# Differential attention in 512-column projections, with two-group turning and six weight low parts on GpSimd

## The chip, the cores and the metric

One core of one Trainium2 chip runs the whole program. The metric is the device time of one execution in microseconds (us). The engines are TensorE (PE; its weight loads are shown apart as PEld), VectorE (DVE), ScalarE (ACT), GpSimd (POOL) and SyncE (SP), which issues the weight transfers.

## What is computed

The program computes one 256-token sequence of width 1024 through three layers: a hybrid layer, then a layer with gated linear attention, then one with differential attention; each of the last two has a gated feed-forward block and a gated embedding step behind it. Only the mixer of the third layer is changed. Cut to that:

```
q, k, v = split(h @ w_in)                      # w_in 1024 x 3072: 1024 columns each
q = rope(rms_norm(q per 64 columns, g_q))      # 8 heads x 2 maps x 64 columns
k = rope(rms_norm(k per 64 columns, g_k))
lam = exp(sum(lam_q1*lam_k1)) - exp(sum(lam_q2*lam_k2)) + lambda_init
pr = softmax(q k^T / 8)                        # two maps for each head
a = pr[0] - lam * pr[1]
o = rms_norm(a @ v per head, g_sub) * (1 - lambda_init)
return o @ w_out                               # w_out 1024 x 1024
```

## The kernel before

All matrix products run at f32 accuracy as three fp32r products. A weight chunk of 1 MB (128 partitions x 2048 values) lands in a slot of RAW. ACT rounds it into WH, the high part (`hi`, line 1129), then DVE subtracts it from RAW into WL, the low part (`lo`, line 1730, two inputs from SBUF). PE then adds high by high, high by low and low by high (`mm3`; line 375 is the matmul of all of them, line 383 the transpose). RAW, WH and WL have three slots each. Chunk c is fetched when both parts of c-3 are made (the `sync_program` loop); its high part waits for the transfer and for PE to have finished c-3 (semaphore `gemm`); PE waits for both parts of c (`ready`).

A few chunks have their low part made by GpSimd instead. They are listed in `POOL_LO` (line 127) and made by the `lo` in `gpsimd_program` (line 2508), in the order of that program: seven in all, among them the second chunk of `ple_w_gate0` just ahead of the stage, and the second chunk of `ffn_w_in1` just behind it. None lies within the stage.

The differential stage is 12 chunks of `diff_w_in` and 4 of `diff_w_out`. Heads are taken in four groups of two. `DIFF_CHUNKS` gives the order of the 12: each is 256 columns wide and all 1024 rows deep (8 blocks of 128), queries (0), keys (1) or values (2) of one group. `toks` runs a chunk as 8 blocks x 2 token halves x 3 products of 256 columns, in two halves of 24 matmuls, into one PSUM bank (0 or 1 in turn; 7 and 3 for the first two). In `toks`, block k of the first chunk first calls `ahead`, which turns block 6 of the normalised input at k = 3 and block 7 at k = 4.

Each engine's order is written out by hand:
- PE (lines 1034 to 1110): chunk halves, between them the turning of queries and keys (`turn_q`, `turn_k`, four transposes each), `scores` of a head (banks 2 and 3), `turn_a` (the weights A of a head turned), `values`, `turn_o` (the output of a group turned) and `back` (a half of a `diff_w_out` chunk); last `down_last`.
- ACT (lines 1630 to 1711): `hi`, `evac` (a projection out of PSUM, scaled by the row's norm, line 1589), `square` (line 1597), `rstd_y` (the norm's root), `turned` (line 1603), `exps` (line 1612), `a_turned`, `out_square`, `out_hi`.
- DVE (lines 2410 to 2494): `lo`; for a group `sums` (line 2319), four `product`s with the cosine and sine tables (line 2335, two SBUF inputs), two `turning`s (line 2340, two SBUF inputs; the second lets PE turn the queries), `factors`, `key_norm` (line 2347; it lets PE turn the keys); for a head `maxima` (line 2352, from PSUM), `coefficients`, `difference` (line 2373); for an output group `out_sums`, `out_factors`, `out_norm` (line 2400, from PSUM), `out_lo` (line 2408, from PSUM). `settled()` makes DVE wait for its own last operation.
- A group's `S` buffer (queries and keys, 1024 columns) alternates between two places.

Scratch: `nm1` is the norm of the stage's input. Its sum waits for ACT's squares, which ACT issues behind the eviction of the turned block 7; its result releases the first `evac`. Then DVE makes lambda (lines 2303 to 2312) with one exponential on ACT (line 1575) in between, and only then `lo` of the stage's third chunk.

Of the kernel before, what the change touches and what calls it, by code (L numbers as in the profile page):

```python
# [65 lines left out]
def weight_chunks():  # L66
# [59 lines left out]
POOL_LO = [AT["w_o_hg"] + 1, AT["w_ff1"] + 1, AT["gla_w_in"] + 1, AT["ffn_w_in0"] + 1, AT["ple_w_gate0"] + 1, AT["ffn_w_in1"] + 1, AT["ple_w_gate1"] + 1]  # L126
# [143 lines left out]
class Diff:  # L270


    def __init__(self, m):
        self.m = m
        self.V = v3(m.ar(2048, 2048), 2)
        self.w = m.ar(6144, 1024), m.ar(7168, 1024)
        tabs = m.ar(14336, 2048)
        self.tab = [tabs[:, 512 * x:512 * x + 512].rearrange("p (n j) -> p n j", j=32) for x in range(4)]

    def S(self, g):  # L280

        return self.m.ar(4096 + 1024 * (g % 2), 1024)
# [17 lines left out]

    def factors(self, h):
# [13 lines left out]
def rope_half(ap, h):  # L315
    return ap.rearrange("p (n a j) -> p n a j", a=2, j=32)[:, :, h, :]
# [53 lines left out]
def tensor_program(e, m):  # L370
# [589 lines left out]
    def chunk(g, sec, half):  # L960
        n = WHEN[g, sec]
        if n >= 4 and half == 0:
            e.wait_ge(s["df_ev"], n - 1)
        toks(d0 + n, n % 2 if n >= 2 else (7, 3)[n], m.pair("X"), None if n else "nm1",
             range(4 * half, 4 * half + 4))

    def turn_q(g):
        e.wait_ge(s["df_r"], g + 1)
        for j in range(2):
            for tb in range(2):  # L970
                i = tr(PS[:, 7, 256 * j + 128 * tb:256 * j + 128 * tb + 128],
                       D.S(g)[:, 256 * tb + 128 * j:256 * tb + 128 * j + 128])
        i.then_inc(s["df_tr"], 1)

    def turn_k(g):
        e.wait_ge(s["df_kn"], g + 1)
        for j in range(2):
            for tb in range(2):
                i = tr(PS[:, 4, 256 * j + 128 * tb:256 * j + 128 * tb + 128],
                       D.S(g)[:, 512 + 256 * tb + 128 * j:512 + 256 * tb + 128 * j + 128])  # L980
# [23 lines left out]
    def values(h):  # L1004
# [3 lines left out]
        if h % 2 == 0:  # L1008
            e.wait_ge(s["df_ev"], WHEN[g, 2] + 1)
# [23 lines left out]

    for g, sec in DIFF_CHUNKS[:4]:
        chunk(g, sec, 0)
        chunk(g, sec, 1)
    chunk(0, 2, 0)
    turn_q(0)
    turn_k(0)
    chunk(0, 2, 1)  # L1040
# [35 lines left out]
    chunk(3, 2, 0)
    e.wait_ge(s["df_qk"], 7)
    turn_a(3)
    values(2)
    scores(7)  # L1080
    chunk(3, 2, 1)
    e.wait_ge(s["df_qk"], 8)
    turn_o(0)
    values(3)
    e.wait_ge(s["df_tlo"], 1)
    turn_a(4)
    e.wait_ge(s["df_at"], 4)
    turn_a(5)
# [12 lines left out]
    e.wait_ge(s["df_at"], 7)  # L1101
    turn_o(2)
# [13 lines left out]
def scalar_program(e, m):  # L1116
# [456 lines left out]
    rstd_y("nm1")  # L1573
    e.wait_ge(s["df_l"], 1)
# [1093 lines left out]
```

## Time and profile before

| what | value |
|---|---|
| median of 3 runs | 1062.19 us (1062.15 to 1062.34) |
| the profiled execution | 1062.51 us, of which the span is 1060.6 us |
| PE busy | 1049.5 us (99%), 6582 matmuls |
| DVE, ACT, POOL busy | 714.8 us (67%), 596.8 us (56%), 57.3 us (5%) |
| granted TensorE clock | 1.0 of full speed in the whole span |
| HBM read | 182.21 MB, 173 GB/s over the span |

The busy time of PE is no measure of how dense its work is, since matmuls overlap and their ends are modelled. The starts of successive matmuls tell the pace. The differential stage lies at 719.6 us to about 841 us of the span, and its last `diff_w_out` chunk begins at about 835.2 us.

### The profile page before, as it was taken

To read this page: it belongs to the slowest core of one execution; us is meant where nothing else is said; L and a number is where in the kernel's file an instruction comes from. 1 tells how busy PE (TensorE), PEld (TensorE's weight loads), DVE (VectorE), ACT (ScalarE), POOL (GpSimd) and SP (SyncE) were. 2 spreads that over 40 slices of the span, in tenths; PEclk is the share of its full clock that TensorE was granted. 3 is DMA by queue.
4 is the path that set the end of the run, shared out by engine and by line. 5 is a ranking of instruction groups with operands and counts; after the bars stand their busy time and mean duration, and the time that the engine had idled before them with its cause. 6 is when DMAs were issued, how large, how long until landed. Compare 5 with 4: busy or idle time off the path is not lost.

```text
span 1060.6 us, 16168 instructions
## 1 busy us (share of the span) xinstructions
PE 1049.5 (99%) x6582; PEld 926.2 (87%) x6582; DVE 714.8 (67%) x835; ACT 596.8 (56%) x754; POOL 57.3 (5%) x53
## 2 busy tenths in 40 slices
PE   9999999999999999999999999999999999999998
PEld 8897999888888889888888888899998888888888
DVE  6547786675656567966666666677888676666564
ACT  7558554454444356865754444476776564444464
POOL 0000001110000030002005000010000200000010
PEclk9999999999999999999999999999999999999999
DMA  8735444646564656345465565555424455555651
GB/s 270 257 120 184 134 159 126 213 137 220 173 221 161 200 162 207 127 128 201 159 198 200 186 210 190 168 173 185 160 81 154 134 185 198 173 199 174 211 171 41
DMA packets 131274, 184.32 MB, mean 174 GB/s; under 512 B 3200, under 2 KB 107904, under 8 KB 131200
## 3 DMA queue, kind: packets, MB, share of 16 engines
q1 hardware_dynamic: 130752, 182.68, 51.9%
q8 instruction: 53, 0.87, 0.3%
q0 software_dynamic: 160, 0.52, 0.2%
q14 instruction: 21, 0.17, 0.0%
q10 hardware_dynamic: 288, 0.07, 0.0%
HBM read 182.21 MB, written 1.05 MB: 173 GB/s over the span
## 4 chain that ended last, share of the span: by engine, by line
PE 90%; DVE 5%; ACT 3%; issue 2%; DMA 1%; SPq 0%; DVEq 0%; ACTq 0%
PE PS L375 88%; PE PS L383 2%; DVE WL L1730 1%; ACT WH L1129 1%; DMA RAW<-in_gla_w_in_dram 0%; DMA H<-in_x_dram 0%; DVE AR L1968 0%; DVE AR L2160 0%; ACT AR L1144 0%; DVE AR L2158 0%; DVE SC L2352 0%; ACT H L1439 0%; ACT X L1138 0%; DVE X L1742 0%; DVE AR L2152 0%
## 5 line engine op out<-in xcount | busy, mean ns | idle before, releaser
L1730 DVE TENSOR_TENSOR WL<-RAW,WH 128x2048 fp32r<-128x2048 f32 (+1 forms) x170 | 375.4, 2211 | 139.1 <-ACT WH L1129 138.6
L1129 ACT ACTIVATE WH<-RAW 128x2048 fp32r<-128x2048 f32 (+1 forms) x177 | 326.3, 1848 | 82.0 <-PE PS L375 77.6
L375 PE MATMUL PS<-WH,X 128*128 128x512 f32 (+1 forms) x1168 | 307.4, 346 | 0.6 <-issue 0.4
L375 PE MATMUL PS<-O,WH 128*128 128x512 f32 (+1 forms) x880 | 265.7, 363 | 0.2 <-DVE WL L1730 0.2
L375 PEld LDWEIGHTS PS<-WH,X 128*128 128x128 f32 x1168 | 204.6, 190 | 28.3 <-issue 2.1
L375 PE MATMUL PS<-X,WH 128*128 128x256 f32 (+1 forms) x864 | 218.2, 331 | 0.5 <-ACT X L1138 0.5
L375 PE MATMUL PS<-O,WL 128*128 128x256 f32 x744 | 203.3, 282 | 0.0
L375 PE MATMUL PS<-WL,X 128*128 128x512 f32 (+1 forms) x584 | 200.7, 344 | 0.0
L375 PEld LDWEIGHTS PS<-O,WH 128*128 128x128 f32 x880 | 156.1, 189 | 25.1 <-issue 0.7
L375 PE MATMUL PS<-X,WL 128*128 128x256 f32 x608 | 167.6, 282 | 0.0
L375 PEld LDWEIGHTS PS<-X,WH 128*128 128x128 f32 x864 | 145.1, 190 | 15.6 <-issue 0.9
L375 PE MATMUL PS<-WH,O 128*128 128x512 f32 (+1 forms) x496 | 142.9, 366 | 0.9 <-issue 0.6
L375 PEld LDWEIGHTS PS<-O,WL 128*128 128x128 f32 x744 | 140.7, 189 | 3.0
L375 PEld LDWEIGHTS PS<-WL,X 128*128 128x128 f32 x584 | 110.7, 190 | 13.0
L375 PEld LDWEIGHTS PS<-X,WL 128*128 128x128 f32 x608 | 115.3, 190 | 1.8
L375 PEld LDWEIGHTS PS<-WH,O 128*128 128x128 f32 x496 | 89.6, 189 | 15.2 <-ACT O L1628 0.7
L1513 ACT ACTIVATE AR<-PS 128x512 f32<-128x512 f32 x44 | 26.3, 597 | 116.5 <-PE PS L375 116.5
L375 PE MATMUL PS<-WL,O 128*128 128x512 f32 (+1 forms) x248 | 90.0, 363 | 0.0
L2508 POOL TENSOR_TENSOR WL<-RAW,WH 128x2048 fp32r<-128x2048 f32 x7 | 32.3, 4621 | 694.6 <-ACT WH L1129 694.6
L375 PE MATMUL PS<-AR 128*64 128x64 f32 (+7 forms) x672 | 58.0, 281 | 2.4 <-DVE AR L1825 1.1
L375 PEld LDWEIGHTS PS<-AR 128*64 128x64 f32 (+3 forms) x672 | 48.8, 165 | 9.1 <-issue 3.3
L375 PEld LDWEIGHTS PS<-WL,O 128*128 128x128 f32 x248 | 46.9, 189 | 7.0
(215 smaller groups left out, 764.0 us busy)
## 6 DMA issues: line engine op xcount, KB each, us to landing
RAW<-in_ffn_w_in_dram SPq DMA_DIRECT2D x44, 1024.0 KB, 5.1
RAW<-in_w_ff_dram SPq DMA_DIRECT2D x32, 1024.0 KB, 5.4
RAW<-in_ffn_w_out_dram SPq DMA_DIRECT2D x22, 1024.0 KB, 5.1
RAW<-in_w_in_dram SPq DMA_DIRECT2D x20, 1024.0 KB, 5.1
RAW<-in_gla_w_in_dram SPq DMA_DIRECT2D x12, 1024.0 KB, 5.3
RAW<-in_diff_w_in_dram SPq DMA_DIRECT2D x12, 1024.0 KB, 5.3
RAW<-in_ple_w_gate_dram SPq DMA_DIRECT2D x8, 1024.0 KB, 5.1
RAW<-in_w_out_dram SPq DMA_DIRECT2D x4, 1024.0 KB, 5.0
```

The lines of the kernel that those rows point to most:

```text
L375: return e.matmul(o, l, r, start=start, stop=stop, skip_group_check=skip)
L383: return e.transpose(o, i, m.con("ident", slice(0, k))[:, 0:k])
L1129: act(high, raw, ACT.Copy).then_inc(s["w_hi"], 1)
L1513: act(v3(m.ar(5632 + 1024 * x + 512 * (i % 2), 512), 2), PS[:, 2 * x:2 * x + 2, 256:512], ACT.Copy).then_inc(s["sw_b"], 1)
L1730: e.tensor_tensor(low, raw, high.bitcast(F32), ALU.subtract).then_inc(s["w_lo"], 1)
L2508: e.tensor_tensor(low, raw, high.bitcast(F32), ALU.subtract).then_inc(s["w_lop"], 1)
```

## The change

1. `DIFF_PAIRS` takes the place of `DIFF_CHUNKS`: a pair is 512 columns (queries, keys or values of two groups), and each of its two chunks holds 512 columns by half of the rows (4 blocks of 128). `toks_long` runs it: chunk x = 0 for both token halves, then x = 1 for both, 12 matmuls of 512 columns each time, into one bank for each token half. There are still 12 chunks of 1 MB.
2. Norms and turning by units of two groups' queries or keys. Orders of the first four pairs: queries 0-1, keys 0-1, queries 2-3, keys 2-3, then the values. `key_norm` runs twice on 1024 columns instead of four times on 512. The scores of head 1 use banks 5 and 6.
3. The low parts of chunks 3, 5, 7, 9, 11 and 13 of the stage (counted from 0, `d0 + n`) move from DVE to GpSimd.
4. The three hand-written orders are new. ACT's `hi` of the stage's chunk 2 moves ahead of the exponential of lambda.

```diff
-            for g, sec in DIFF_CHUNKS:
-                wide("diff_w_in", sec * 1024 + 256 * g)
+            for sec, x in DIFF_PAIRS:
+                long("diff_w_in", sec * 1024 + 512 * x)
...
+DIFF_PAIRS = ((0, 0), (1, 0), (0, 1), (1, 1), (2, 0), (2, 1))
...
+POOL_LO = [AT["w_o_hg"] + 1, AT["w_ff1"] + 1, AT["gla_w_in"] + 1, AT["ffn_w_in0"] + 1, AT["ple_w_gate0"] + 1,
+           *(AT["diff_w_in"] + n for n in (3, 5, 7, 9, 11, 13)), AT["ffn_w_in1"] + 1, AT["ple_w_gate1"] + 1]
...
@@ tensor_program @@
+    def pair(n, x, tb):
+        def free(tb):
+            if n >= 2:
+                e.wait_ge(s["df_ev"], 2 * n - 1 + tb)
+        toks_long(d0 + 2 * n + x, x, (0, 1) if n else (7, 3), m.pair("X"), (tb,), None if n else "nm1", free)
+    def turn(g, sec):
+        if sec:
+            e.wait_ge(s["df_kn"], g // 2 + 1)
+        else:
+            e.wait_ge(s["df_r"], g // 2 + 1)
...
+    pair_rest(0, *ALL)
+    pair_rest(1, *ALL)
+    pair(2, 0, 0)
+    turn(0, 0)
+    pair(2, 0, 1)
+    pair(2, 1, 0)
+    e.wait_ge(s["df_qk"], 1)
+    turn(1, 0)
+    pair(2, 1, 1)
+    pair(3, 0, 0)
+    turn(0, 1)
+    pair(3, 0, 1)
+    e.wait_ge(s["df_qk"], 3)
+    turn(1, 1)
+    scores(0)
+    scores(1)
+    turn(2, 0)
+    pair(3, 1, 0)
...
+    turn(3, 0)
+    pair(5, 0, 0)
+    turn(2, 1)
...
+    turn_o(0)
+    pair(5, 1, 1)
+    turn_a(5)
+    scores(7)
+    back(0, 0)
...
@@ scalar_program @@
     rstd_y("nm1")
+    hi(AT["diff_w_in"] + 2)
     e.wait_ge(s["df_l"], 1)
     act(m.sc("ls")[:, 0:2], m.sc("ls")[:, 0:2], ACT.Exp).then_inc(s["df_lx"], 1)
...
-    hi(d0 + 2)
     evac(0, 0)
     hi(d0 + 3)
-    hi(d0 + 4)
     evac(0, 1)
     square(0)
+    hi(d0 + 4)
+    rstd_y("dq0")
+    hi(d0 + 5)
     evac(1, 0)
-    hi(d0 + 5)
-    rstd_y("dq0")
     hi(d0 + 6)
     evac(1, 1)
...
@@ vector_program @@
     lo(d0 + 2)
-    lo(d0 + 3)
+    sums(0)
+    products(0)
+    factors(0)
+    turning(0, 0)
+    turning(0, 1)
     lo(d0 + 4)
...
     lo(d0 + 6)
     sums(1)
+    products(1)
+    turning(1, 0)
     factors(1)
     turning(1, 1)
     key_norm(1)
     sums(2)
+    products(2)
     factors(2)
     turning(2, 0)
+    turning(2, 1)
+    maxima(0)
+    maxima(1)
+    lo(d0 + 8)
...
@@ gpsimd_program, behind lo(POOL_LO[4]) @@
+    for n in (3, 5, 7, 9, 11, 13):
+        lo(AT["diff_w_in"] + n)
     e.wait_ge(s["df_o"], 8)
     p_rows(1)
```

## Rows read from the trace of the kernel before

**Rows 1.** The page: busy time of the engines; the chain that ended last, by engine.

```profile
PE 1049.5 (99%) x6582; PEld 926.2 (87%) x6582; DVE 714.8 (67%) x835; ACT 596.8 (56%) x754; POOL 57.3 (5%) x53
...
PE 90%; DVE 5%; ACT 3%; issue 2%; DMA 1%; SPq 0%; DVEq 0%; ACTq 0%
```

**Rows 2.** Windows, stage (window: us; then busy us of each engine, clock, DMA).

```profile
729.60:744.00 14.40, 14.22 (x119) 14.05 (x118) 13.83 (x17) 9.15 (x13) 0.00 (x0) 1.00 0.69 218
...
sum 115.60, PE 112.95 PEld 105.01 DVE 98.90 ACT 79.59 POOL 0.74; mean PE 14.12 PEld 13.13 DVE 12.36 ACT 9.95 POOL 0.09
```

**Rows 3.** The chain of waits, stage (start us, us, what).

```profile
804.37 2.20 DVE WL L1730
...
807.82 2.29 DVE WL L1730
810.11 0.61 DVE O L2408
810.77 1.09 PE PS L383 x8
...
832.71 6.83 PE PS L375 x30
```

**Rows 4.** The chain of waits: 48 matmuls of 256 columns at the stage's head.

```profile
713.68 5.76 PE PS L375 x48
```

**Rows 5.** PE's timeline, `toks_long` earlier: 512 columns, 33 matmuls between these starts.

```profile
430.34 0.62 PE L375 MATMUL PS<-WH,O 128*128 128x512 f32 x2
...
437.82 0.62 PE L375 MATMUL PS<-WH,O 128*128 128x512 f32 x2
```

**Rows 6.** PE's timeline: block 7 is turned (start us, us, engine, line).

```profile
722.88 0.38 PE L383 MATMUL PS<-CON,H 128*128 128x128 f32 x2
```

**Rows 7.** ACT's timeline, stage's head.

```profile
727.63 1.90 ACT L1129 ACTIVATE WH<-RAW 128x2048 fp32r<-128x2048 f32 x1
```

**Rows 8.** DVE's timeline, stage's head.

```profile
698.98 0.15 DVE L1768 TENSOR_TENSOR SC<-SC 128x2 f32<-128x2 f32 x1
...
726.29 0.16 DVE L1753 SCALAR_TENSOR_TENSOR SC<-SC 128x2 f32<-128x2 f32 x1
...
729.62 2.29 DVE L1730 TENSOR_TENSOR WL<-RAW,WH 128x2048 fp32r<-128x2048 f32 x1 [1.45 <-ACT WH L1129]
```

**Rows 9.** GpSimd's low part, whole trace: shortest, median, longest ns.

```profile
L2508 POOL TENSOR_TENSOR WL<-RAW,WH x7: 4611/4623/4627, 174.4 to 1029.0; 128x2048 fp32r<-128x2048 f32 x7
```

**Rows 10.** GpSimd's timeline: four products just ahead of DVE's row below.

```profile
394.12 5.05 POOL L2533 TENSOR_TENSOR HS<-H,AR 128x512 f32<-128x512 f32 x4
```

**Rows 11.** DVE's timeline, beside GpSimd's four products.

```profile
398.40 0.79 DVE L1768 TENSOR_TENSOR SC<-SC 128x2 f32<-128x2 f32 x1
```

**Rows 12.** GpSimd's 32 small table products, shortest, median, longest ns.

```profile
L2548 POOL TENSOR_TENSOR AR<-SML,CON x32: 313/322/2416, 569.5 to 585.3; 128x64 f32<-128x64 f32 x32
```

**Rows 13.** DVE's timeline, beside GpSimd's table products.

```profile
570.64 2.49 DVE L1730 TENSOR_TENSOR WL<-RAW,WH 128x2048 fp32r<-128x2048 f32 x1 [1.19 <-ACT WH L1129]
573.49 2.29 DVE L1730 TENSOR_TENSOR WL<-RAW,WH 128x2048 fp32r<-128x2048 f32 x1 [0.36 <-ACT WH L1129]
...
578.40 0.92 DVE L2254 TENSOR_TENSOR AR<-AR,RB 128x512 f32<-128x512 f32 x1
```

**Rows 14.** Groups by line, DVE in the stage: busy us, mean ns.

```profile
L2335 DVE TENSOR_TENSOR AR<-AR 128x512 f32<-128x512 f32 x16 | 10.1, 687 | 0.0
L2352 DVE TENSOR_REDUCE SC<-PS 128x4 f32<-128x1024 f32 x8 | 9.8, 1223 | 2.9 <-PE PS L375 2.7
...
L2340 DVE TENSOR_TENSOR AR<-AR 128x512 f32<-128x512 f32 x8 | 5.5, 688 | 0.1
L2319 DVE TENSOR_REDUCE SC<-AR 128x16 f32<-128x1024 f32 x4 | 4.9, 1214 | 1.3 <-ACT AR L1597 1.3
```

**Rows 15.** One tensor: the weight transfers of `diff_w_in`.

```profile
DMA to landing us min/median/max: 5.1/5.3/6.3
```

**Rows 16.** One line: ACT's exponentials, shortest, median, longest ns.

```profile
L1612 ACT ACTIVATE AR<-PS,SC x32: 546/562/596, 753.4 to 811.3; 128x256 f32<-128x256 f32 x32
```

More of the change, by code:

```diff
@@ L958, in tensor_program @@
     d0 = AT["diff_w_in"]
[L960 to L968, printed above, removed]
+    def pair(n, x, tb):
[8 more added lines that the diff above has]
+            e.wait_ge(s["df_r"], g // 2 + 1)
         for j in range(2):
             for tb in range(2):
[L971 to L980, printed above, removed]
+                i = tr(PS[:, (7, 4)[sec], 256 * j + 128 * tb:256 * j + 128 * tb + 128],
+                       D.block(g, sec)[:, 256 * tb + 128 * j:256 * tb + 128 * j + 128])
         i.then_inc(s["df_tr"], 1)
     def scores(h):
-        g = h // 2
+        g, b = h // 2, D.banks(h).start
         Q, K = (v3(D.QK(g)[:, 512 * i:512 * i + 512], 2) for i in range(2))
-        e.wait_ge(s["df_qk"], 2 * g + 2)
-        if h >= 1:
-            e.wait_ge(s["df_e"], 2 * h)
+        e.wait_ge(s["df_qk"], D.turns(g, 1))
+        if h >= 2:
+            e.wait_ge(s["df_e"], 2 if h == 2 else 2 * h)
         for tb in range(2):
@@ L1032, in back, with pair_rest @@
              lambda tb: e.wait_ge(*((s["df_e"], 16) if tb else (s["df_ev"], 12))), (half,))
[L1034 to L1040, printed above, removed]
+    def pair_rest(n, *parts):
+        for x, tb in parts:
+            pair(n, x, tb)
+    ALL = (0, 0), (0, 1), (1, 0), (1, 1)
+    pair_rest(0, *ALL)
[4 more added lines that the diff above has]
+    pair(2, 1, 0)
@@ L1072, in tensor_program @@
+    pair(5, 0, 0)
+    turn(2, 1)
+    values(0)
+    values(1)
+    e.wait_ge(s["df_qk"], 7)
+    turn(3, 1)
+    scores(4)
+    pair(5, 0, 1)
+    e.wait_ge(s["df_qk"], 8)
+    turn_a(2)
+    turn_a(3)
+    scores(5)
+    pair(5, 1, 0)
     e.wait_ge(s["df_at"], 3)
-    turn_k(3)
-    values(1)
+    turn_a(4)
+    values(2)
+    values(3)
     scores(6)
[L1076 to L1079, printed above, removed]
+    e.wait_ge(s["df_at"], 5)
+    turn_o(0)
+    pair(5, 1, 1)
@@ L1080, in tensor_program @@
+    turn_a(5)
     scores(7)
[L1081 to L1088, printed above, removed]
     back(0, 0)
     values(4)
-    back(0, 1)
+    values(5)
     e.wait_ge(s["df_at"], 6)
     turn_o(1)
-    values(5)
+    back(0, 1)
+    e.wait_ge(s["df_tlo"], 1)
+    turn_a(6)
     back(1, 0)
-    turn_a(6)
+    e.wait_ge(s["df_at"], 7)
+    turn_o(2)
     e.wait_ge(s["df_tlo"], 2)
@@ L2328, in product, with factors @@
-    def product(g, j):
-        S = D.S(g)
+        mean_square(f"dq{u}", m.sc(f"dq{u}.ss"), 1.0 / 64)
+    def factors(u):
+        r, (sec, x) = rstd_r(f"dq{u}"), DIFF_PAIRS[u]
+        if sec == 0:
+            e.tensor_scalar(nq[:, 16 * x:16 * x + 16], r, 0.125, None, ALU.mult).then_inc(own.up(), 1)
+    def product(u, j):
+        sec = DIFF_PAIRS[u][0]
+        S = D.S(sec)
         if j == 0:
-            e.wait_ge(s["df_ev"], WHEN[g, 1] + 1)
+            e.wait_ge(s["df_ev"], 2 * u + 2)
@@ L2343, in key_norm @@
-    def key_norm(g):
-        k = v3(D.S(g)[:, 512:1024], 8)
+        i = e.tensor_tensor(rope_half(D.S(sec), j), rope_half(w1, j), rope_half(w2, j), ALU.add if j else ALU.subtract)
+        i.then_inc(*((s["df_r"], 1) if j and sec == 0 else (own.up(), 1)))
+    def key_norm(u):
+        k = v3(D.S(1), 16)
         settled()
-        e.wait_ge(s["df_r"], g + 1)
-        e.tensor_tensor(k, k, m.sc(f"dq{g}.r")[:, 8:16].unsqueeze(2).to_broadcast([128, 8, 64]), ALU.mult).then_inc(s["df_kn"], 1)
+        e.tensor_tensor(k, k, m.sc(f"dq{u}.r").unsqueeze(2).to_broadcast([128, 16, 64]), ALU.mult).then_inc(s["df_kn"], 1)
@@ L2351, in maxima @@
         e.wait_ge(s["df_sc"], h + 1)
[L2352 removed]
+        e.tensor_reduce(c, PS[:, D.banks(h), :].rearrange("p x (t k) -> p (x t) k", t=2), AX, ALU.max).then_inc(own.up(), 1)
         settled()
@@ L2479, in vector_program @@
     out_norm(1)
+    maxima(7)
+    lo(d0 + 14)
     difference(6)
-    coefficients(7)
-    lo(d0 + 14)
-    difference(7)
+    out_sums(2)
     out_lo(1)
-    out_sums(2)
     out_factors(2)
     out_norm(2)
+    head(7)
     lo(d0 + 15)
```

258 lines of the change are left out of this document (105 added, 153 removed).

## The prediction, made before the changed kernel was run

> **What bounds the kernel now.** I read the page first. PE is busy 99% and carries 90% of the chain that ended last [rows 1], so a gain has to come out of PE's own time or its waits in this stage, and any wait that the change gives PE counts in full. The windows cut the stage out, from its first projection at 719.6 us to the start of its last `diff_w_out` chunk at 835.2 us: 115.6 us, in which PE stands still for 115.60 - 112.95 = 2.65 us, and DVE, though it is 67% busy overall, works 98.90 us. At the stage's head DVE works 13.83 of 14.4 us [rows 2]. DVE is the second bound here: at 804 to 811 us the chain of waits leaves PE and runs through two low parts and an output's low part on DVE before PE goes on [rows 3].
>
> **Projections.** 12 chunks x 48 = 576 matmuls of 256 columns become 288 of 512. 48 of 256 columns take 5.76 us, 120.0 ns each [rows 4]; with 512 columns 33 take 437.82 - 430.34 = 7.48 us, 226.7 ns each [rows 5]. So 69.1 us become 65.3 us: -3.8 us, all on PE's path. The scores, values and turnings are the same in number.
>
> **The head of the stage.** `toks_long` takes blocks 0 to 3 for both token halves before block 4, so input block 7 is turned behind 24 matmuls of 226.7 ns, at 725.6 us (5.4 us, with the turning of block 6 and the wait ahead of it 0.5 more), where it now stands at 722.88 [rows 6]: 2.7 us later. The input's norm hangs on ACT's squares behind that turned block. ACT's high part of chunk 2, which began at 727.63 us [rows 7], now goes ahead of the exponential, at 728.4 us, and ends at 730.3. DVE's norm result moves from 726.45 to 729.1 us, its lambda work with it, and the exponential ends at 730.5; behind that and two small operations comes the low part of chunk 2, 731.0 to 733.2 us, where it began at 729.62 [rows 8]. PE has finished chunks 0 and 1 at 731.2 and starts chunk 2 at 733.4: **+2.2 us**.
>
> **DVE.** Six low parts of 2.29 us leave it: 13.7 us of 98.9. Products, turnings and norms keep their elements; two `key_norm`s of 1024 columns for four of 512 are no more work. If nothing else happened, I lay the queues on (products 2.5 us for four, maxima 1.4 us, exponentials 2.2 us a head, a transfer 5.3 us) and find PE's 2.65 us of waits gone, and two of 0.3 us behind exponentials (`scores` of heads 5 and 7). The sum without contention is -3.8 - 2.65 + 2.2 + 0.55 = **-3.7 us**.
>
> **GpSimd's low parts and the port.** One takes 4.62 us, in all seven cases [rows 9]. By time alone that is hidden: a chunk's high part is there about 9 us before PE needs it. But rows show the two engines excluding each other. GpSimd ran four products of 1.3 us from 394.12 to 399.17 us [rows 10]. A DVE operation on two columns began at 398.40 beside the last of them and took 0.79 us, to 399.19 [rows 11]; the same line takes 0.15 us at 698.98 [rows 8]. The other way about, GpSimd's table products take 322 ns as a rule and up to 2416 ns [rows 12], about a whole DVE low part plus their own time, and DVE's low parts and a product beside them took 2.49 and 0.92 us for 2.29 and 0.69 [rows 13]. So where both read two SBUF operands, the later one waits for the whole of the other. All the seven long low parts of the kernel before lie where DVE reads PSUM; the six new ones lie in the middle of its SBUF work. The Trainium skill, page "SBUF — State Buffer", section "Who interferes with whom", states it so too: a VectorE instruction with two SBUF inputs contends with a GpSimd instruction that reads SBUF, and the second to issue blocks fully. That speaks against this change.
>
> So six low parts take 27.7 us of the port where DVE would have taken 13.7 us. Products, turnings, norms, differences, the small norm steps and the remaining low parts need it; maxima and sums (1.22 and 1.21 us [rows 14]), output norms and PSUM low parts don't. What hides GpSimd is thus only some 27 us of such DVE work, if it happens to lie there.
>
> **The queues with the port**, each taking it when it comes first:
> 1. Chunk 3's low part, 733.3 to 737.9. The first `products` wait for it (they could start at 735.7) and run 737.9 to 740.4; `factors` follow. Chunk 5's high part (its transfer takes 5.3 us [rows 15], and it waits for PE's chunk 2) ends at 740.8, in the middle of `factors`, whose small steps leave gaps: GpSimd holds the port 741.0 to 745.7. The two `turning`s and the low part of chunk 4, all queued behind, end at 749.4. PE wants chunk 4 at 744.3: **+5.2 us**.
> 2. Chunk 7's low part (757.3 to 762.0) finds DVE waiting for a root; `factors`, `turning` and `key_norm` of the first keys end at 764.5, PE wants to turn them at 764.0: +0.6.
> 3. Chunk 9's comes at 769.8, within 0.2 us of the gap between the two `turning`s of the second queries. If it gets in, PE waits 4.9 us for them, if not 0.5; but then chunk 11's falls ahead of `factors(3)` and `maxima(3)`, the exponentials of head 3 (2.2 us, four of 562 ns less their overlap [rows 16]) are late, ACT's eviction of the first values is queued behind them, and PE waits 4.5 instead of 1.1. Either way some **+5.5 us**.
> 4. Chunk 13's (808 to 813) delays the first output's norm, then head 6's maxima and exponentials, for which `turn_o(0)` and `scores(7)` wait: 1.3 each, **+2.6**.
> Sum +13.9, against the 3.7 gained: +10.2 us. Behind this PE's remaining `diff_w_out` work is as before.
>
> Who gets the port when both want it no row shows between long operations. If DVE keeps it through its small gaps, step 1 costs 0.7 (chunk 5's low part waits to 744.8), but chunk 7's gets in during a sum and the first keys are 3.6 late; the following ones cost 2.8, 1.3 and about 0.5, sum 8.5 to 9: +5 us. These are the ends, +5 and +10; below a half of either nothing excludes a luckier interleaving. That a 322 ns product of GpSimd got in ahead of DVE's low part [rows 13] is nearest to first come, first served, so I take +8.
>
> The profiled execution took 1062.51 us (1060.6 of span and 1.9 around it), 0.3 above the median of 1062.19. I forecast 1070.2 for the median: 1062.2 + 8.
>
> **Rivals.**
> - *The low parts are hidden and the port costs nothing* (long instructions let the other in between, or both happen to interleave). For it: DVE had 98.9 us of work and would have 85. Against it: the 0.79 us and 2416 ns rows. Then -3.7: 1058.5 us, faster. The point from which it decides: DVE's work on SBUF operands lengthened by under 1.5 us for each low part. Chance 0.2.
> - *DVE keeps the port in small gaps*, +5: 1067 us. PE's largest wait is then that for the first keys, about 759.5, and chunk 4 is nearly on time. Chance 0.3.
> - *Partial hiding*: only one or two of the listed waits come about, 3 to 6 us, and give back what was won: 1060 to 1064. Chance 0.15.
> - *The head alone*: the projections gain nothing because the pace is not that of 512 columns. I see no reason; the same helper has that pace in rows 5. It would add 3.8 to any case; 0.02.
> - The forecast, port in turn as they come, 1068 to 1073: chance 0.33.
>
> **Numbers.** The range leaves out what is above 1072.5 and below 1058.2, about 2 in 10 with what I have missed. The likeliest case has 1067 to 1072.5. 0.2% is 2.1 us, about what a measurement of this kernel can tell. Faster by more (under 1060.1): the first rival and a little of the third, 0.2. Within: 0.12. Slower: 0.68.
>
> **What the profile after would show.** Right: matmuls of 512 columns 227 ns apart in the stage; PE idle at 731 to 733 for the low part of chunk 2; GpSimd's low parts start some 0.2 us behind ACT's high parts, or late behind a DVE operation; and DVE instructions of the product, turning or low-part lines that take 3 to 5 us where they took 0.7 or 2.3, with PE waiting for DVE's low part of chunk 4 and for turned queries or keys. The stage up to its last `diff_w_out` chunk then takes 120 to 126 us where it took 115.6. Wrong: DVE's durations stay at 0.69 and 2.29 us beside GpSimd's, and the stage takes about 112 us.

## The result, and the profile after

| kernel | median | against before, 95% interval |
|---|---|---|
| before | 1062.19 us | |
| changed | 1073.42 us (1071.45 to 1074.1, 5 runs) | 1.0101 [1.0086, 1.0116] |
| changed, the profiled execution | 1071.45 us, of which the span is 1069.6 us | |

The change makes the kernel 11.2 us slower, by the medians. I had forecast 1070.2 us with a range of 1058.2 to 1072.5: the side was right, and the time fell outside the range. The profiled execution is the shortest of the five, 8.9 us over the profiled one of before, and the trace accounts for that much.

The page of the changed kernel: the busy time of the engines, the chain that ended last by engine, and GpSimd's low parts (thirteen where there were seven).

```profile
PE 1051.1 (98%) x6294; PEld 914.3 (85%) x6294; DVE 717.6 (67%) x825; ACT 595.6 (56%) x742; POOL 87.1 (8%) x59
...
PE 90%; DVE 6%; ACT 2%; issue 1%; DVEq 0%; ACTq 0%
...
L2513 POOL TENSOR_TENSOR WL<-RAW,WH 128x2048 fp32r<-128x2048 f32 x13 | 62.1, 4775 | 781.8 <-ACT WH L1146 781.8
```

PE still carries 90% of the chain [rows 1], with 288 matmuls fewer. DVE lost six low parts of 2.29 us and gained 2.8 us of busy time: something took 13.7 + 2.8 = 16.5 us of DVE. (The chain's 6% of DVE were 5%.)

Windows of the changed kernel over the stage (us; busy us of PE, PE's weight loads, DVE, ACT and POOL; PEclk; DMA share; GB/s):

```profile
729.60:744.00 14.40, 12.57 (x49) 9.91 (x48) 12.34 (x18) 9.47 (x11) 6.08 (x2) 0.88 0.48 147
...
758.50:773.00 14.50, 12.55 (x69) 9.87 (x68) 14.05 (x21) 7.23 (x9) 5.26 (x2) 1.00 0.24 74
773.00:787.80 14.80, 12.40 (x58) 9.43 (x57) 12.54 (x24) 13.19 (x33) 0.58 (x1) 0.88 0.61 211
...
811.00:835.20 24.20, 21.67 (x124) 18.08 (x124) 20.93 (x54) 17.18 (x41) 0.92 (x1) 0.93 0.27 88
...
sum 124.70, PE 114.07 PEld 92.33 DVE 101.64 ACT 78.16 POOL 30.48; mean PE 12.67 PEld 10.26 DVE 11.29 ACT 8.68 POOL 3.39
```

To the start of its last `diff_w_out` chunk the stage takes 124.7 us where it took 115.6 [rows 2]: +9.1, inside the 120 to 126 that I gave. PE stands still for 124.70 - 114.07 = 10.63 us where it was 2.65, +8.0 us. And the third column from the end, PEclk, holds what I had not reckoned with: the granted clock is 0.88, 0.88 and 0.93 in three windows, where the kernel before has 1.0 throughout.

PE's timeline of the changed kernel where it had stood still (start, length, line, instruction, and in brackets the idle time ahead of it and what ended it):

```profile
733.04 0.47 PE L390 MATMUL PS<-WH,X 128*128 128x512 f32 x1 [1.83 <-DVE WL L1745]
...
762.17 0.66 PE L398 MATMUL PS<-CON,AR 128*128 128x128 f32 x4 [1.81 <-DVE AR L2365]
...
775.00 1.14 PE L390 MATMUL PS<-AR 64*128 64x256 f32 x8 [0.77 <-ACT AR L1632]
777.76 0.74 PE L390 MATMUL PS<-WH,X 128*128 128x512 f32 x1 [1.63 <-ACT AR L1610]
...
794.89 0.47 PE L390 MATMUL PS<-WH,X 128*128 128x512 f32 x1 [1.80 <-ACT AR L1610]
...
814.41 0.70 PE L390 MATMUL PS<-AR 64*128 64x256 f32 x4 [2.53 <-ACT AR L1632]
```

These are 10.4 of the 10.63 us. What made them late is on DVE and GpSimd. GpSimd's timeline of the changed kernel, its six low parts, and then DVE's timeline, the six instructions that took longer than the same line takes elsewhere (and the four products of L2353, which took their usual time, ahead of the third of them):

```profile
732.73 4.60 POOL L2513 TENSOR_TENSOR WL<-RAW,WH 128x2048 fp32r<-128x2048 f32 x1 [38.28 <-ACT WH L1146]
742.52 6.08 POOL L2513 TENSOR_TENSOR WL<-RAW,WH 128x2048 fp32r<-128x2048 f32 x1 [5.19 <-ACT WH L1146]
753.87 5.13 POOL L2513 TENSOR_TENSOR WL<-RAW,WH 128x2048 fp32r<-128x2048 f32 x1 [5.26 <-ACT WH L1146]
767.74 4.76 POOL L2513 TENSOR_TENSOR WL<-RAW,WH 128x2048 fp32r<-128x2048 f32 x1 [8.74 <-ACT WH L1146]
787.22 4.61 POOL L2513 TENSOR_TENSOR WL<-RAW,WH 128x2048 fp32r<-128x2048 f32 x1 [14.72 <-ACT WH L1146]
807.37 4.55 POOL L2513 TENSOR_TENSOR WL<-RAW,WH 128x2048 fp32r<-128x2048 f32 x1 [15.54 <-ACT WH L1146]
```

```profile
735.54 1.82 DVE L1778 TENSOR_SCALAR SC<-SC 128x16 f32<-128x16 f32 x1
...
747.93 2.84 DVE L1745 TENSOR_TENSOR WL<-RAW,WH 128x2048 fp32r<-128x2048 f32 x1 [3.78 <-ACT WH L1146]
...
752.03 2.50 DVE L2353 TENSOR_TENSOR AR<-AR 128x512 f32<-128x512 f32 x4
754.57 4.99 DVE L2359 TENSOR_TENSOR AR<-AR 128x512 f32<-128x512 f32 x1
...
769.22 3.31 DVE L2373 SCALAR_TENSOR_TENSOR SC<-SC 128x4 f32<-128x4 f32 x1
...
788.39 3.46 DVE L2373 SCALAR_TENSOR_TENSOR SC<-SC 128x4 f32<-128x4 f32 x1
...
808.00 3.94 DVE L2373 SCALAR_TENSOR_TENSOR SC<-SC 128x4 f32<-128x4 f32 x1
```

The two lists belong together. L2359 is a `turning`, a sum or difference of two products, 0.69 us as a rule; beside GpSimd's third low part it took 4.99, and 754.57 + 4.99 = 759.56 while GpSimd's 753.87 + 5.13 = 759.00. That low part began beside the products, which ended at 752.03 + 2.50 = 754.53, and it was ahead of the turning, which began 0.04 us later. L2373 is a step on 4 columns behind the maxima, 0.17 us by itself; three times it began inside a GpSimd low part and ended with it (769.22 + 3.31 = 772.53, GpSimd's 767.74 + 4.76 = 772.50; the same at 791.85 and 811.94). Less what they take by themselves, the six were held for 1.65 + 0.55 + 4.30 + 3.14 + 3.29 + 3.77 = 16.7 us: that is the 16.5 of the page. GpSimd is held too: its second low part, begun at 742.52 inside DVE's own (741.86 to 744.15), took 6.08 us. One of the six has a single input from SBUF: L1778, a TENSOR_SCALAR on 16 columns, began at 735.54 inside the first low part and ended with it (737.36 and 737.33), where it takes 0.17 us elsewhere. The sum just ahead of it, a TENSOR_REDUCE with one input, ran beside the same low part in its usual 1.22 us. So "two SBUF operands", as the prediction has it, is too narrow by at least this instruction. On the way to PE: the keys' norm is late at 762; at 769 and 788 the exponentials are late, ACT's evictions are queued behind them, and PE wants the bank (777.76 and 794.89, L1610 is the eviction); at 808 group 7's exponentials are late (814.41).

The clock, in windows of 1 us around the first wait (same columns):

```profile
732.00:733.00 1.00, 0.00 (x0) 0.00 (x0) 0.89 (x1) 1.00 (x2) 0.27 (x1) 1.00 0.00 0
...
734.00:735.00 1.00, 1.00 (x4) 0.71 (x4) 0.71 (x1) 1.00 (x2) 1.00 (x1) 0.50 0.85 82
735.00:736.00 1.00, 1.00 (x4) 0.81 (x3) 0.97 (x2) 1.00 (x1) 1.00 (x1) 0.50 0.99 344
...
737.00:738.00 1.00, 1.00 (x6) 0.82 (x5) 1.00 (x3) 0.43 (x2) 0.34 (x1) 1.00 0.54 207
```

0.50 is the lower of TensorE's two levels, 1.2 GHz. It begins soon after PE's wait of 1.83 us has ended, and the clock is full again in the window from 737 on. The same happens at about 777.8 to 781.2 and at 815.3 to 818.8, behind the waits that ended at 777.76 and 814.41. Mean clocks of 0.88 over 14.4 us, 0.88 over 14.8 and 0.93 over 24.2 are (1.73 + 1.78 + 1.69) = 5.2 us of PE's work not done, the third term of the sum: -3.8 (the pace of 512 columns) + 8.0 (standing still) + 5.2 = +9.4, against the +9.1 of the windows and the +8.9 of the execution.

### The profile page after: what moved, and what is told of

It reads as the page before. It is cut to its first block, busy times and chain, and to the rows that moved or that the text cites. A ratio compares the mean times of both kernels' runs of the same rounds, so it can differ in the third digit from the quotient of the medians.

```text
span 1069.6 us, 15574 instructions
## 1 busy us (share of the span) xinstructions
PE 1051.1 (98%) x6294; PEld 914.3 (85%) x6294; DVE 717.6 (67%) x825; ACT 595.6 (56%) x742; POOL 87.1 (8%) x59
## 4 chain that ended last, share of the span: by engine, by line
PE 90%; DVE 6%; ACT 2%; issue 1%; DVEq 0%; ACTq 0%
PE PS L390 88%; PE PS L398 2%; DVE SC L2373 1%; ACT AR L1632 1%; DVE WL L1745 1%; DVE AR L2359 1%; ACT WH L1146 1%; DVE AR L2353 0%; DVE SC L2370 0%; DVE AR L1983 0%; ACT AR L1161 0%; DVE SC L2335 0%; ACT X L1155 0%; DVE X L1757 0%; DVE AR L1811 0%
## 5 line engine op out<-in xcount | busy, mean ns | idle before, releaser
L1745 DVE TENSOR_TENSOR WL<-RAW,WH 128x2048 fp32r<-128x2048 f32 (+1 forms) x164 | 362.3, 2211 | 141.1 <-ACT WH L1146 140.6
L390 PE MATMUL PS<-WH,X 128*128 128x512 f32 (+1 forms) x976 | 300.3, 383 | 5.7 <-ACT AR L1610 3.4
L390 PEld LDWEIGHTS PS<-WH,X 128*128 128x128 f32 x976 | 181.9, 191 | 41.3 <-issue 6.1
L390 PE MATMUL PS<-WL,X 128*128 128x512 f32 (+1 forms) x488 | 185.5, 380 | 0.0
L2513 POOL TENSOR_TENSOR WL<-RAW,WH 128x2048 fp32r<-128x2048 f32 x13 | 62.1, 4775 | 781.8 <-ACT WH L1146 781.8
L390 PEld LDWEIGHTS PS<-WL,X 128*128 128x128 f32 x488 | 93.1, 191 | 16.7
```

The costliest lines, as they stand in the source:

```text
L390: return e.matmul(o, l, r, start=start, stop=stop, skip_group_check=skip)
L1745: e.tensor_tensor(low, raw, high.bitcast(F32), ALU.subtract).then_inc(s["w_lo"], 1)
L2513: e.tensor_tensor(low, raw, high.bitcast(F32), ALU.subtract).then_inc(s["w_lop"], 1)
```

## The experiments

All ratios are against the kernel before, run on the same chip beside each, and compare means; differences in us are of medians. The medians of the kernel before in all these pairs lie between 1062.19 and 1062.60 us, so differences between runs of different pairs are good to some 0.4 us.

**1. The changed kernel with zeros in place of GpSimd's six low parts.** GpSimd waits for the same semaphores and fills WL by two memsets, 0.95 us. The six chunks' products with the low part are thus products with zeros.

```diff
     for n in (3, 5, 7, 9, 11, 13):
-        lo(AT["diff_w_in"] + n)
...
+        e.memset(low[:, 0:1024].bitcast(F32), 0.0)
+        e.memset(low[:, 1024:2048].bitcast(F32), 0.0).then_inc(s["w_lop"], 1)
```

> The changed kernel, but GpSimd fills the six low parts with zeros (two fills of 1024 columns each) instead of subtracting: it reads nothing from SBUF. The low parts of six chunks are thus left out of the result. Port theory: VectorE's products, turnings and small norm steps keep 0.69 and 0.17 us beside GpSimd's fills (each about 0.95 us, two for a low part); what is left is the wait at the head (1.8 us) with its 1.7 us at the lower clock, so the sum without contention, -3.7, plus 1.7: about 1060 us, 13 us faster than the changed kernel. Rival (the wide pairs and the new order make the waits, whoever makes the low parts): within 2 us of the changed kernel's 1073.4.

Measured: 1058.15 us, 0.9965 [0.9952, 0.9978]. So GpSimd's six subtractions cost the changed kernel 1073.42 - 1058.15 = 15.3 us, and what is left of the change gives 4.0 (4.5 against the kernel before beside it). DVE's timeline of this run, the turning and the step behind the maxima, each beside a fill:

```profile
754.28 0.69 DVE L2359 TENSOR_TENSOR AR<-AR 128x512 f32<-128x512 f32 x1
...
766.95 0.16 DVE L2373 SCALAR_TENSOR_TENSOR SC<-SC 128x4 f32<-128x4 f32 x1
```

They took 0.69 and 0.16 us, against 4.99 and 3.31 above. The Trainium skill, page "SBUF — State Buffer", section "Who interferes with whom", has VectorE instructions with two SBUF inputs contend with GpSimd instructions that read SBUF, not with such as only write; the trace agrees, as a fill, which only writes, held none of the steps with two inputs. (Run 8 shows a fill holding a step with one.) The five runs fall apart by clock: 1057.9 to 1058.2 at 1.0 of full speed, 1059.61 at 0.998, 1060.72 at 0.997. The run at 0.998 is the profiled one, with a single stretch at the half clock, from 733 to 737 us: here one stretch costs 1.6 us, by the whole program's time. The zeros are also ready 2.7 us sooner than a subtraction; that this is not what the run gains from is shown by run 7, where the low parts are ready later and most of the loss is gone all the same.

**2. The changed kernel with all low parts on DVE.** The six `lo` calls go from GpSimd's program into DVE's, behind `lo(d0 + 2)`, `lo(d0 + 4)`, `key_norm(1)`, `maxima(2)`, `head(3)` and `maxima(6)`.

```diff
-           *(AT["diff_w_in"] + n for n in (3, 5, 7, 9, 11, 13)), AT["ffn_w_in1"] + 1, AT["ple_w_gate1"] + 1]
+           AT["ffn_w_in1"] + 1, AT["ple_w_gate1"] + 1]
...
     lo(d0 + 2)
+    lo(d0 + 3)
     sums(0)
...
```

> The changed kernel with all low parts of the stage on VectorE again, each placed where its high part is ready. Port theory: six times 2.29 us are back on VectorE (13.7 us), but no instruction is stretched, GpSimd is idle in the stage, and TensorE loses little beyond the head: 1060 to 1064 us. Rival (VectorE's load is what bounds the stage in this order): TensorE waits for low parts or for turned queries, 1068 us or more. Rival (order alone): 1071 to 1074.

Measured: 1061.89 us, 0.9991 [0.9981, 1.0]. The rest of the change, the 512 columns with the new orders, is worth 0.3 us here (0.7 against the kernel before beside it): PE still waits 1.85 us at the head (733.64), 1.01 for exponentials (797.13) and 1.50 for an eviction (811.19). Against this run the changed kernel pays 11.5 us for having its six low parts on GpSimd.

**3. The kernel before with its odd low parts on GpSimd.** Nothing else of the change.

```diff
     lo(POOL_LO[4])
+    for n in (3, 5, 7, 9, 11, 13):
+        lo(AT["diff_w_in"] + n)
```

> The kernel before, with one part of the change alone: the low parts of the stage's chunks 3, 5, 7, 9, 11 and 13 on GpSimd, in the old 256-column chunks and the old orders. Port theory: slower than before by 4 to 12 us, with VectorE instructions of 3 to 5 us beside GpSimd's low parts. Rival (the move relieves VectorE, and the loss comes from the wide pairs): 1060 to 1062 us, since 13.7 us leave VectorE at a stage that has it busy for 98.9 of 115.6 us.

Measured: 1079.01 us, 1.0151 [1.0136, 1.0166]: +16.4 us over the 1062.6 beside it. That is more than the 4 to 12 I had expected. The old orders and chunks lose by the move too, so the loss is not one of the wide pairs. (The 16.4 is to be set beside the 11.5 of run 2, both against low parts made by DVE, and not beside the 15.3 of run 1, which is against zeros.) DVE's timeline of this run has the same prints: a low part, four products, two turnings, and steps on 16 and on 4 columns. The step on 16 is again the TENSOR_SCALAR with one input.

```profile
734.29 4.99 DVE L1730 TENSOR_TENSOR WL<-RAW,WH 128x2048 fp32r<-128x2048 f32 x1 [2.09 <-ACT WH L1129]
...
740.55 6.93 DVE L2335 TENSOR_TENSOR AR<-AR 128x512 f32<-128x512 f32 x4
...
759.38 5.69 DVE L2340 TENSOR_TENSOR AR<-AR 128x512 f32<-128x512 f32 x2
...
774.43 4.51 DVE L1763 TENSOR_SCALAR SC<-SC 128x16 f32<-128x16 f32 x1
...
795.53 3.79 DVE L2355 SCALAR_TENSOR_TENSOR SC<-SC 128x4 f32<-128x4 f32 x1
```

**4. The changed kernel with only the head mended.** Chunk 2's high and low part stand ahead of the turned block 7 and the norm.

```diff
-    turn_hi("nm1", 6, 7)
+    turn_hi("nm1", 6)
+    hi(AT["diff_w_in"] + 2)
+    turn_hi("nm1", 7)
...
-    hi(AT["diff_w_in"] + 2)
...
     turn_lo("nm1", 6, 7)
+    lo(AT["diff_w_in"] + 2)
     rows_rstd("nm1", ("nm1_r", 1))
...
-    lo(d0 + 2)
     sums(0)
```

> The changed kernel with only its head mended: ScalarE makes the high part of chunk 2 between the evictions of input blocks 6 and 7, VectorE its low part before the input's norm. TensorE's wait of 1.83 us at 733 us goes, and if the halved clock from 733.4 to 736.5 us is the consequence of that wait, its 1.7 us too: 3.5 us less, about 1069 to 1070 us against 1073.4 (1068 against the fastest). If the clock falls for another reason: 1071.5. The later port waits may fall otherwise, by 2 us either way.

Measured: 1075.72 us, 1.0124 [1.0109, 1.0139]. The wait at 733 is gone and the kernel is 2.3 us slower. GpSimd's and DVE's timelines of this run, and PE's at the longest wait of all:

```profile
741.53 4.58 POOL L2514 TENSOR_TENSOR WL<-RAW,WH 128x2048 fp32r<-128x2048 f32 x1 [2.48 <-ACT WH L1146]
```

```profile
739.00 2.48 DVE L2355 TENSOR_TENSOR AR<-AR 128x512 f32<-128x512 f32 x4
741.41 0.16 DVE L1765 TENSOR_TENSOR SC<-SC 128x16 f32<-128x16 f32 x1
741.61 4.54 DVE L1767 SCALAR_TENSOR_TENSOR SC<-SC 128x16 f32<-128x16 f32 x1
746.18 0.17 DVE L1769 SCALAR_TENSOR_TENSOR SC<-SC 128x16 f32<-128x16 f32 x1
...
747.93 4.49 DVE L1746 TENSOR_TENSOR WL<-RAW,WH 128x2048 fp32r<-128x2048 f32 x2
```

```profile
750.32 0.77 PE L390 MATMUL PS<-WH,X 128*128 128x512 f32 x1 [5.42 <-issue]
```

This is step 1 of the prediction's queue, which the changed kernel itself did not show. DVE's small steps of `factors` follow each other at 0.2 us; the one at 741.41 ended at 741.57, GpSimd's low part began at 741.53, and the step that began at 741.61 took 4.54 us where the next took 0.17. The 40 ns between the rows of two dependent steps were enough for GpSimd, as they were in the changed kernel at 754.53. The low part of chunk 4, queued behind the turnings, is the first of the two that begin at 747.93, made by 750.2, and PE, which waited 5.42 us, goes on at 750.32 (the bracket says "issue" and names no engine; the low part's end and the matmul's start agree). In the changed kernel's profile PE ran its chunk 2 at the half clock; ACT's high part of chunk 5 waits for that chunk, and GpSimd came at 742.52, behind DVE's turnings instead of ahead of them. That the one follows from the other is read from the two timelines; no run isolates it.

**5 and 6. All on DVE with the head mended; then two moves at the tail as well.** Run 6 puts chunk 12's low part behind `maxima(4)`, and ACT's `evac(5, 1)` ahead of a norm's root.

```diff
     lo(d0 + 11)
-    lo(d0 + 12)
     maxima(4)
+    lo(d0 + 12)
...
     weights(6)
-    rstd_y("df1")
     evac(5, 1)
+    rstd_y("df1")
```

> All low parts on VectorE as in the run above, and the head mended as in the head run. Port theory: with GpSimd idle nothing can be held up by it, so mending the head now gives its 1.8 us of wait, and 1.7 us more in runs in which the clock fell behind it: 1061.9 becomes 1058.5 to 1060. Rival (the head's wait only moves on to the next low part, as it did with GpSimd): TensorE waits for chunk 3's low part at about 737 us instead, and the time stays within 1 us of 1061.9.

> As the one above, with the low part of chunk 12 behind head 4's maxima (they stood 1 us late, and the scores of head 5 with them) and the last values' eviction ahead of a norm's root on ScalarE (TensorE waited 1.5 us for it at 811 us, and 1.6 us more went to the clock). Expected another 2 to 4 us less: 1055.5 to 1058, faster than the kernel before by 0.4 to 0.6%. If the waits only move: as the one above.

Measured: 1062.58 us, 1.0003 [0.9994, 1.0012], and 1061.59 us, 0.999 [0.9981, 0.9999]. Both missed what I hoped for. The head's wait had only moved. PE's timeline of run 5:

```profile
744.99 0.47 PE L390 MATMUL PS<-WH,X 128*128 128x512 f32 x1 [2.40 <-ACT WH L1146]
```

The bracket names ACT's high part, but that of chunk 4's low part is the later one: DVE makes it at 742.6 to 744.9, behind the turnings. Run 6 keeps this wait (2.39 us), loses the two of 1.00 and 1.49 us later in the stage, and has one of 1.27 us at 815.61 for group 7's exponentials.

**7. The changed kernel with each of GpSimd's low parts in eight pieces of 256 columns.**

```diff
-        lo(AT["diff_w_in"] + n)
+        for j in range(8):
+            k = slice(256 * j, 256 * j + 256)
+            i = e.tensor_tensor(low[:, k], raw[:, k], high[:, k].bitcast(F32), ALU.subtract)
+        i.then_inc(s["w_lop"], 1)
```

> The changed kernel with each of the six GpSimd low parts cut into eight pieces of 256 columns (about 0.6 us each). Port theory with the port held for one instruction: no VectorE instruction is stretched by more than about 0.7 us where it was by up to 4.3, GpSimd's low part itself takes longer than 4.6 us beside VectorE's work (6 to 10 us), and the time falls from 1073.4 to 1060 to 1067 us. Rival (the port is shared by bandwidth, or GpSimd keeps it between its back-to-back instructions): stretches of 3 to 5 us stay and the time is within 2 us of 1073.

Measured: 1063.47 us, 1.001 [1.0001, 1.0019], 10 us less than the changed kernel for the same work on the same engine in the same order. GpSimd's timeline of this run, the first two of its low parts, and DVE's beside the first:

```profile
733.35 6.50 POOL L2563 TENSOR_TENSOR WL<-RAW,WH 128x256 fp32r<-128x256 f32 x8 [38.29 <-ACT WH L1146]
743.13 9.76 POOL L2563 TENSOR_TENSOR WL<-RAW,WH 128x256 fp32r<-128x256 f32 x8 [3.27 <-ACT WH L1146]
```

```profile
736.16 0.74 DVE L1778 TENSOR_SCALAR SC<-SC 128x16 f32<-128x16 f32 x1
736.82 4.19 DVE L2353 TENSOR_TENSOR AR<-AR 128x512 f32<-128x512 f32 x4
```

GpSimd's low parts take 6.50 and 9.76 us, and DVE's four products 4.19 instead of 2.49. The step on 16 columns took 0.74 us, about one piece, where a whole low part held it 1.82. So the port is held for the length of one instruction, and between pieces the other engine gets in. The clock, 0.998 to 1.0, does not tell these ten runs apart: those at 0.998 took 1063.1 to 1063.8 us and those at 1.0 1063.2 to 1063.9, so here a stretch at the half clock does not show in the whole time.

**8. Zeros and the head mended**, runs 1 and 4 together.

> GpSimd fills zeros in place of the six low parts (left out of the result, as in the first run) and the head is mended: the change as it would be if GpSimd's work cost VectorE nothing and the head's wait were gone. 1058.1 less 1.8: about 1056 us, and no run with the clock below 1.00 in 729 to 744 us. If TensorE's wait only moves on: 1058.

Measured: 1058.61 us, 0.9969 [0.9957, 0.9982]: no better than run 1, and PE waits 2.33 us at 744.7 for chunk 4's low part, as in run 5, here with no subtraction of GpSimd in the stage. That wait is the order's. GpSimd's and DVE's timelines of this run hold one thing more:

```profile
739.95 0.96 POOL L2562 MEMSET WL<- 128x1024 f32 x1 [3.78 <-ACT WH L1146]
```

```profile
740.30 0.63 DVE L2345 TENSOR_SCALAR SC<-SC 128x16 f32<-128x16 f32 x1
```

This step on 16 columns, with one input from SBUF, began inside a fill and ended with it (740.93 and 740.91), where it takes 0.17 us as a rule; the three steps with two inputs ahead of it, two of them beside the fill, kept 0.17 to 0.18. A fill can thus hold this kind of step. It cost at most 0.5 us, once.

**9 and 10. Order mended further; then one low part back to GpSimd in pieces.** Run 9 is run 6 with three moves.

```diff
@@ scalar_program @@
     rstd_y("nm1")
+    hi(AT["diff_w_in"] + 3)
     e.wait_ge(s["df_l"], 1)
...
     evac(0, 0)
-    hi(d0 + 3)
     evac(0, 1)
@@ vector_program @@
     lo(d0 + 3)
     sums(0)
+    lo(d0 + 4)
     products(0)
...
     coefficients(6)
+    maxima(7)
     out_factors(1)
     out_norm(1)
-    maxima(7)
```

> All low parts on VectorE, the head and the tail mended, and three more moves: on ScalarE chunk 5's high part stands ahead of lambda's exponential, on VectorE chunk 4's low part stands ahead of the products and the turnings, and the maxima of group 7 stand ahead of the last normalization of the outputs. No low part is on GpSimd, so no port is shared. If the two waits left in the run before (2.39 us at 744.9 for chunk 4's low part, 1.27 us at 815.6 for group 7's exponentials) came from the order of the work: both go, 1061.6 - 2.4 - 1.3 = 1057.9 us, and 1056 to 1058 if a stretch at the half clock (1.6 us) goes with one of them. If VectorE's sum of work is what holds TensorE up and waits only move on: a wait of 1 to 3 us shows later in the stage and the time stays at 1060 to 1062 us.

(The high part moved is that of chunk 3; the text above has 5.)

> The run beside it with one change: chunk 13's low part is made by GpSimd in eight pieces of 256 columns, beside groups 6 and 7. If VectorE's sum of work late in the stage is what is short: 2.3 us of VectorE go, and the time falls by 0.5 to 2 us against the run beside it. If the order alone was the matter and the port is shared piece by piece: VectorE's small operations there last up to 0.7 us instead of 0.2, some 4 us of stretching against 2.3 us saved, and the time is the same or up to 2 us longer.

Measured: 1056.52 us (1056.47 to 1056.71), 0.9943 [0.9929, 0.9957], and 1057.33 us, 0.995 [0.9937, 0.9962]. Run 9 beats the kernel before, 1062.48 beside it, by 6.0 us and the changed one by 16.9. The sum of run 9's windows over the stage (they end at 830.0, some 0.7 us into the last chunk, by its pattern of matmuls):

```profile
sum 110.40, PE 109.85 PEld 89.62 DVE 97.77 ACT 78.48 POOL 0.74; mean PE 15.69 PEld 12.80 DVE 13.97 ACT 11.21 POOL 0.11
```

PE stands still for 110.40 - 109.85 = 0.55 us, the granted clock is 1.0 in every window, and -3.8 - 2.65 + 0.55 = -5.9 is what the medians show. Giving DVE's chunk 13 to GpSimd, even in pieces, takes 0.8 us back, with a wait of 1.19 us for exponentials at 806.17.

**11 and 12. Run 9 with one, and with all six, whole low parts on GpSimd.**

> The kernel with the mended orders, with chunk 13's low part alone made by GpSimd, as one instruction of 2048 columns. If a GpSimd instruction holds the port for its whole length and comes in at the first gap: one small operation of VectorE beside it takes 3 to 4.6 us instead of 0.2, the exponentials behind it are late, and the time is 1058 to 1060 us, 1 to 3 us over the 1056.5 of the order without it and above the 1057.3 of the eight pieces. If late in the stage there is slack enough: 1056 to 1057 us.

> The kernel with the mended orders, with all six low parts on GpSimd again, each one instruction, as in the changed kernel. If the port is the whole price and better orders hide none of it: 1056.5 + 15.3 (what six low parts cost in the changed kernel over the zeros: 1073.4 - 1058.1) = 1072 us. If the order decides how much of each held operation reaches TensorE, and chunk 4's low part, now ahead of the products and turnings, no longer waits behind them: some 5 us less, 1065 to 1068 us. If the loss came from the order alone: 1057 us or less, since VectorE has 13.7 us less to do.

Measured: 1060.15 us, 0.9977 [0.9967, 0.9987], and 1071.83 us, 1.009 [1.0073, 1.0107]. One whole low part costs 3.6 us and six cost 1071.83 - 1056.52 = 15.3, against the same low parts made by DVE. I had expected 1072 by adding run 1's 15.3, which is counted from zeros; the two rest on different grounds, so their agreement confirms nothing. Like against like, the move costs 16.4 us in the kernel before, 11.5 in the changed kernel and 15.3 in the mended order. GpSimd's, DVE's and PE's timelines of run 11:

```profile
795.81 4.80 POOL L2519 TENSOR_TENSOR WL<-RAW,WH 128x2048 fp32r<-128x2048 f32 x1 [100.99 <-ACT WH L1146]
```

```profile
796.11 1.22 DVE L2372 TENSOR_REDUCE SC<-PS 128x4 f32<-128x1024 f32 x1
797.36 3.27 DVE L2375 SCALAR_TENSOR_TENSOR SC<-SC 128x4 f32<-128x4 f32 x1
800.56 0.15 DVE L1765 TENSOR_TENSOR SC<-SC 128x4 f32<-128x4 f32 x1
```

```profile
803.12 0.49 PE L390 MATMUL PS<-AR 64*128 64x256 f32 x2 [2.78 <-ACT AR L1634]
```

One GpSimd instruction and one step on 4 columns that took 3.27 us for 0.17 are the cause: DVE's maxima, read from PSUM, ran beside GpSimd at their usual 1.22 us, the step behind them was held to 800.6, and PE waited 2.78 us for the exponentials. This profiled execution took 1059.05 us at a clock of 1.0, 2.6 us over run 9's; the other eight, at 0.998, took 1059.9 to 1060.3.

In run 12 my middle theory fell. The windows' largest wait is again at the queries:

```profile
749.51 0.33 PE L398 MATMUL PS<-CON,AR 128*128 128x128 f32 x1 [4.21 <-DVE AR L2361]
```

Chunk 4's low part no longer waits behind the turnings, so the turnings wait behind it and behind GpSimd, beside whose second low part the four products took 6.91 us for 2.49: PE waits 4.21 us in place of the 5.42 of run 4. The mended order is worth 1061.89 - 1056.52 = 5.4 us with the low parts on DVE and 1073.42 - 1071.83 = 1.6 with them on GpSimd: with GpSimd's 27.7 us in the stage it changes which operation is late more than how much is lost.

## Why the prediction was right or wrong

**What bounds, projections.** Right. PE's stretches of projections in the stage, each from its first matmul to what follows, sum to 71.4 us in the kernel before and 67.2 in run 9: -4.2 for -3.8. Run 9 also shows PE's own time and its waits to be what there was to win, 6.0 of the 6.45 us that the pace and the old waits make.

**The head.** Right: 1.83 us at 733.04 behind DVE's low part, for 2.2 at 733.4. But I priced it as a wait alone. It was followed by a stretch at the half clock, another 1.7.

**The sum without contention.** -3.7, so 1058.5; run 1 measured 1058.15. Right, though from parts that differ: of the two waits of 0.3 us one came (0.25 us at 808.95), and two of the five runs lost clock.

**The port.** The mechanism was right, and both reads of the rows [rows 10 to 13] hold: each engine waits for the whole of the other's instruction, in the order in which they come. The condition was drawn too narrowly: a step with one SBUF input, a TENSOR_SCALAR, was held as well (1.82 us for 0.17 in the changed kernel, 4.51 in run 3). The steps, as predicted and as measured in the changed kernel:

| step | predicted | measured in the profile |
|---|---|---|
| 1, chunk 4's low part | 5.2 | 0; 5.42 in run 4 |
| 2, first keys | 0.6 | 1.81 |
| 3, chunks 9 and 11 | 5.5 | 0.77 + 1.63 + 1.80 = 4.2 |
| 4, chunk 13 | 2.6 | 2.53 |
| half clock, three stretches | not in the sum | 5.2 |
| sum | 13.9 | 13.7 |

The sum was right to 0.2 us with one term of 5.2 in it that did not come and one of 5.2 missing that did; that is luck, and the runs tell the two apart. In step 3 I had the turnings or `maxima` as alternatives; it was the step behind the maxima both times, and again in step 4 and in runs 3, 11 and 12. It reads SBUF just behind an operation that reads PSUM, beside which GpSimd can start.

**The step that failed** is the choice of the size, "so I take +8", together with a term put at nothing. Against my own queue, which gave +10.2 (1072.4), I shaded toward "DVE keeps the port in small gaps", which no row showed. The gaps of 40 ns at 754.53 in the changed kernel and at 741.57 in run 4, at both of which GpSimd got in, exclude it. The bound above was also too near: first come, first served was taken as the far end, +10, and the range's 1072.5 left no room for a term that the trace of before could not show. The clock is that term: 5.2 us in the profiled execution, in which the waits that I had listed for the port came to 8.5 us for 13.9. The profiled execution of the kernel before runs at 1.0 throughout (the longest wait of PE in its stage, 1.36 us at 810.77, was not followed by the lower level), so its profile gave no price for it. (Of the 63 executions of the kernel before beside the experiments three ran at 0.998 and took 1063.2 us.)

**The rivals.** "The port costs nothing" fell at its own point: DVE's operations were lengthened by 16.5 / 6 = 2.75 us for each low part, over the 1.5 stated. "DVE keeps the port", +5, fell with the 4.99 us of L2359, begun 0.04 us behind a product. A part of its sign, chunk 4 on time and a wait for the first keys, did come (0 and 1.81 us), but chunk 4 was on time for another reason: the half clock at the head had moved chunk 5's high part behind the turnings, as far as the timelines tell. Partial hiding fell too; three of four steps came. The pace was that of 512 columns.

**What stays open.** The median is 2 us above the profiled execution. By their clocks the five runs of the changed kernel fall in two groups, 1071.45 and 1071.99 at 0.995, 1073.4 to 1074.1 at 0.996 and 0.997: the longer runs lost less clock, so they must have stood still longer, perhaps by chunk 4's wait of run 4; no trace shows one of them, so this is a guess. And which waits are followed by the half clock is not settled. In the changed kernel those of 1.83, 0.77 + 1.63 and 2.53 us were, those of 1.81 and 1.80 us were not. In run 2 a wait of 1.50 us was and one of 1.85 was not; run 4's 2.15 us at 739.2, run 5's 2.40 and run 11's 2.78 were not, and in run 4's wait of 5.42 us the clock fell before the wait had ended. Their length alone does not sort them.

## What to carry to other kernels

Before work moves from VectorE to GpSimd, lay out not their busy times but the time for which each instruction that needs the port keeps the other off. Here those were instructions with two SBUF operands and the small TENSOR_SCALAR steps, and not the reductions, from SBUF or from PSUM. A GpSimd instruction of 4.6 us costs up to 4.6 us to whatever small VectorE step comes in its way, and that step is often the one TensorE waits for. If it has to be moved, cut it into pieces; otherwise leave it, and look for the wait in the order of the queues, where most of the gain was here (5.4 us from run 2 to run 9). And a wait given to TensorE can cost more than its length, so a range should have room for it.

## What the hardware showed that I had not expected

- A low part of 4.6 us got in ahead of VectorE where the rows of two dependent steps lie about 40 ns apart (run 4), and made a step on 16 columns take 4.54 us.
- A TENSOR_SCALAR on 16 columns with one SBUF input was held by GpSimd's subtractions (1.82 and 4.51 us for 0.17) and once by a fill (0.63 us, run 8).
- Stretches at the half clock behind some waits of TensorE of 1.5 us and more, each about 3.4 us long and 1.7 us of its work, which showed as 1.6 us in run 1's time and not at all in run 7's. They come in some executions of one and the same kernel and not in others: run 2's ten runs took 1060.2 to 1060.9 us at 0.999 to 1.0 and 1061.7 to 1062.5 at 0.998, with one of 1063.94 at 0.997. Run 9, with no wait over 0.3 us in the stage, spreads by 0.24 us in all.
- Cutting GpSimd's instruction into eight made its low parts longer, 5.6 to 9.8 us for 4.6 to 6.1, and still gave back 10 us of the 15.3 counted from zeros.
